# Expert outputs through DRAM by token instead of TensorE spreading, paced zero fill, and two panels split ahead of each item

## The chip, the cores and the metric

The kernel runs on one core of a Trainium2 chip. The metric is the device time of one execution in microseconds, in the median of several runs. TensorE (PE) multiplies, VectorE (DVE) and ScalarE (ACT) prepare operands and read results out of PSUM, SyncE (SP) issues most transfers, GpSimd (POOL) issues a few, and 16 DMA engines move the data between HBM and the on-chip memory SBUF.

## The reference

The program is a chain of four layers on 256 tokens of width 1024. The first block has two layers: a hybrid mixer (RWKV-7 scan, two convolutions, gated and summed) with a layer norm, then in layer 0 a dense SwiGLU of inner width 2816 and in layer 1 a mixture of eight experts, each with a layer norm behind it. The second block has two attention layers, each with a squared-ReLU MLP. All of it is float32. The part that the change touches is the mixture of experts:

```python
def _moe_swiglu(x, w_router, w_gate, w_up, w_down):
    logits = (xf @ w_router).astype(jnp.float32)
    top_logit, top_idx = lax.top_k(logits, TOP_K)          # TOP_K = 2
    top_w = jax.nn.softmax(top_logit, axis=-1)
...
    def expert_block(args):
        xs, e = args
        return (jax.nn.silu(xs @ w_gate[e]) * (xs @ w_up[e])) @ w_down[e]

    yb = lax.map(expert_block, (xb, block_expert))
    y_rows = yb.reshape(n_rows, d) * row_weight[:, None].astype(x.dtype)
    out = jnp.zeros_like(xf).at[row_token].add(y_rows)
```

Each token's output is thus the sum of two expert rows, each times its softmax weight. It is added to ALPHA times the token and goes into a layer norm.

## The kernel before

**Precision.** A float32 product is made of three matmuls in a faster format: each operand is written as a high part and a low part, and hi·hi, lo·hi and hi·lo are added in PSUM (`mm3`, lines 1205 to 1211; its first product goes through `mm`, line 364). ACT makes the high part of a weight panel with a copy ("widens" it, line 2005), DVE subtracts it for the low part ("splits" it, line 2850), and PE may use the panel then.

**Panels.** All weights lie in DRAM as 460 panels of 128 x 2048 numbers, 1 MiB each. SP loads them in order of use. In the experts' part there are seven places for raw panels (three in `ring`, three in `ring_more`, one in `xT`) and four for high parts (three in `ring_hi`, one in `xT_hi`). A place is free for the next panel when the counter `panel_used` has passed the panel that was in it; PE raises the counter with the first matmul of the panel that follows.

**Dense feed-forward of layer 0** (about 300 to 472 us). It uses a ring of three places only: a panel is loaded, cast and split by DVE (lines 2951 and 2953) and used. One chunk is three panels: gate, up and down. At its start POOL writes zeros into the DRAM buffer `routed_x` (line 3399), in one DMA of 6 MiB.

**Experts of layer 1** (about 802 to 1590 us). The tokens of an expert are handled in items of up to 128 rows; the number of items is found on the chip, and this input has 8. One item takes 33 panels: for each of 11 chunks two gate-up panels of 12 matmuls each (`wide`), and one down panel of 12 matmuls (`last`). The order is 0,0,1,1,2,2,down 0,3,3,down 1 and so on. Between the two gate-up panels of chunk s PE turns the hidden tile of chunk s-1 (`turn`). Near the end of an item, in chunk 10, PE also turns the 128 token rows of the next item (`turn_next`), which SP has fetched from `routed_x`, and the next item's `in_slot` one-hot tile, which says what token belongs in which row. ACT and DVE then make `xe_hi` and `xe_lo` of them.

**Outputs of an item before the change.** The down products end in banks 2 and 3. ACT copies them to `y_hi` (line 2024, two halves), DVE makes `y_lo` (line 2871), and PE multiplies them with the one-hot tile `spread` (`scatter`, lines 1331 and 1332): four matmuls of 512 columns for the first half after the first chunk of the next item, four for the second half in chunk 3. That puts the rows of the item at their tokens. DVE adds each result times the token's weight to `acc` (line 2877, four operations of 512 columns an item). The last item's are spread after the loop.

**What each engine does at an item's beginning.** The item body of PE, ACT and DVE is a hardware loop over the first 7 items, followed by a copy of the body for the last one. ACT's body starts with widening gate-up panel 1 (the second of chunk 0), then the first half of the outputs, panel 2, a one-element Silu that brings in the table set, the second half of the outputs, panel 3, and the `silu` of chunk 0. DVE's splits follow the same order. The instruction stream has an ACT_TABLE_LOAD at two places of the loop's body: ahead of its first copy, and ahead of the one-element Silu.

**The start of the experts' part.** DVE computes the routing, loads two numbers into registers, and makes `one_hot`. PE gathers item 0's tokens with it (`gather`, line 1308). DVE then computes the rows in `routed_x` to which each token goes (`route_rows`), sets `acc` to ALPHA times the tokens, and splits panel 0. POOL scatters the tokens into `routed_x` with four indirect DMAs. ACT widens panel 0 beside the gather, panel 1 only as the first thing of the item loop.

## Time and profile before

| | us |
|---|---|
| median of 3 runs | 2289.98 |
| lowest, highest | 2286.58, 2302.31 |
| profiled execution, its own time | 2287.82 |
| span of its profile | 2285.8 |
| PE busy (share of the span) | 2234.8 (98%) |
| DVE busy | 1811.1 (79%) |
| ACT busy | 1058.9 (46%) |
| POOL busy | 13.7 (1%) |
| TensorE clock granted, mean | 0.992 |

The span runs from the first to the last instruction in the profile. The engines wait for each other by semaphores; an idle time is put down to what released it. Matmuls overlap: a matmul of 512 columns is shown as 0.39 us long, while the next one starts about 0.23 us after it. So the distance between two starts is the cost, and a busy share of 98% does not mean that PE has no time to lose.

### The profile page before, as it was taken

What the parts mean: (1) busy time and instruction counts of PE and PEld (TensorE: products, weight loads), DVE (VectorE), ACT (ScalarE), POOL (GpSimd) and SP (SyncE); (2) the same over time, 40 slices, a digit from 0 to 9 for tenths busy, and PEclk for the clock granted to TensorE, in tenths of its full rate; (3) what the DMA queues carried; (4) which work ended last, traced back from release to release, by engine and by line L of the source; (5) the groups of instructions that cost most, each with busy time, mean ns of one, the idle gap of its engine ahead of it and who ended that gap; (6) DMA issues with size and microseconds to landing.
All of it is one profiled execution on the core that took longest, in us unless ns stands there. A gap on an engine that the chain in (4) does not pass through costs nothing.

```text
span 2285.8 us, 39519 instructions
## 1 busy us (share of the span) xinstructions
PE 2234.8 (98%) x15724; PEld 1937.8 (85%) x15724; DVE 1811.1 (79%) x1989; ACT 1058.9 (46%) x1257; POOL 13.7 (1%) x20
## 2 busy tenths in 40 slices
PE   9999999999999999999999999999999999999999
PEld 8999889989899878878788787877888999888998
DVE  4885777778866698988989889897878877578776
ACT  5435410034445377776877768775464100243000
POOL 0000000000000000000000000000000000000000
PEclk9999999999999999999999999999999999999999
DMA  5333465533334499999999999996512555322554
GB/s 209 122 113 115 162 255 206 185 145 130 113 112 148 194 372 347 357 362 359 362 344 380 343 361 354 355 374 239 204 72 75 185 186 189 140 93 94 192 191 149
DMA packets 71903, 507.80 MB, mean 222 GB/s; under 512 B 7808, under 2 KB 7936, under 8 KB 12400
## 3 DMA queue, kind: packets, MB, share of 16 engines
q1 hardware_dynamic: 68240, 489.77, 57.7%
q0 software_dynamic: 3552, 16.44, 1.9%
q8 instruction: 84, 1.38, 0.2%
q14 instruction: 27, 0.22, 0.0%
HBM read 496.74 MB, written 9.44 MB: 221 GB/s over the span
## 4 chain that ended last, share of the span: by engine, by line
PE 80%; DVE 9%; ACT 5%; DMA 3%; issue 2%; DVEq 0%; SPq 0%; ACTq 0%
PE wide L364 27%; PE wide L1210 22%; PE wide L1211 22%; DMA ring<-in_weights 2%; DVE ring_lo L2342 2%; ACT mix_hi L1736 1%; PE wide L1547 1%; DVE ring_lo L2953 1%; PE wide L1291 1%; ACT ring_hi L2005 1%; PE wide L1031 1%; PE wide L1533 1%; DVE ring_hi L2951 0%; ACT xe_hi L2019 0%; PE wide L1023 0%
## 5 line engine op out<-in xcount | busy, mean ns | idle before, releaser
L364 PE MATMUL wide<-ring_hi,hT_hi 128*128 128x512 f32 x664 | 263.6, 397 | 7.4 <-DVE ring_lo L2953 4.2
L1211 PE MATMUL wide<-ring_hi,hT_lo 128*128 128x512 f32 x664 | 261.8, 394 | 0.0
L2850 DVE TENSOR_TENSOR ring_more_lo<-ring_more,ring_hi 128x2048 fp32r<-128x2048 f32 x96 | 219.8, 2290 | 43.6 <-ACT ring_hi L2005 42.0
L364 PE MATMUL wide<-mix_xT_hi,mix_hi 128*128 128x256 f32 x816 | 238.4, 292 | 12.6 <-DVE ring_lo L2342 9.7
L364 PE MATMUL wide<-xT_hi,ring_hi 128*128 128x256 f32 x864 | 243.3, 282 | 3.0 <-DVE xT_lo L2336 1.6
L1961 ACT ACTIVATE gate_s<-wide 128x512 f32<-128x512 f32 x43 | 25.8, 600 | 474.4 <-PE wide L1211 474.4
L1211 PE MATMUL wide<-xT_hi,ring_lo 128*128 128x256 f32 x864 | 242.8, 281 | 0.0
L1210 PE MATMUL wide<-xT_lo,ring_hi 128*128 128x256 f32 x864 | 242.5, 281 | 0.0
L2850 DVE TENSOR_TENSOR ring_lo<-ring,ring_hi 128x2048 fp32r<-128x2048 f32 x96 | 219.7, 2289 | 23.1 <-ACT ring_hi L2005 22.0
L1211 PE MATMUL wide<-mix_xT_hi,ring_lo 128*128 128x256 f32 x832 | 234.4, 282 | 0.0
L1210 PE MATMUL wide<-xT_lo,mix_hi 128*128 128x256 f32 x816 | 230.4, 282 | 0.0
L364 PE MATMUL wide<-ring_hi,xe_hi 128*128 128x512 f32 x544 | 218.8, 402 | 1.4 <-DVE ring_more_lo L2850 1.1
L2953 DVE TENSOR_TENSOR ring_lo<-ring,ring_hi 128x2048 fp32r<-128x2048 f32 x94 | 215.5, 2293 | 3.2
L2342 DVE TENSOR_TENSOR ring_lo<-ring,mix_hi 128x2048 fp32r<-128x2048 f32 x60 | 137.3, 2288 | 101.1 <-ACT mix_hi L1736 100.7
L1211 PE MATMUL wide<-ring_hi,xe_lo 128*128 128x512 f32 x544 | 214.9, 395 | 0.0
L1210 PE MATMUL wide<-ring_lo,hT_hi 128*128 128x512 f32 x536 | 210.3, 392 | 0.0
L2005 ACT ACTIVATE ring_hi<-ring_more 128x2048 fp32r<-128x2048 f32 x96 | 184.3, 1920 | 51.2 <-PE wide L364 50.0
L2005 ACT ACTIVATE ring_hi<-ring 128x2048 fp32r<-128x2048 f32 x96 | 184.1, 1917 | 30.5 <-PE wide L364 30.5
L2951 DVE CAST ring_hi<-ring 128x2048 fp32r<-128x2048 f32 x94 | 115.3, 1227 | 102.9 <-DMA ring<-in_weights 102.9
L364 PEld LDWEIGHTS wide<-mix_xT_hi,mix_hi 128*128 128x128 f32 x816 | 155.1, 190 | 22.4 <-DVE ring_lo L2342 16.0
L364 PEld LDWEIGHTS wide<-xT_hi,ring_hi 128*128 128x128 f32 x864 | 163.2, 189 | 6.5 <-DVE ring_lo L2953 2.7
L1210 PEld LDWEIGHTS wide<-xT_lo,ring_hi 128*128 128x128 f32 x864 | 162.8, 188 | 1.6
(545 smaller groups left out, 4941.5 us busy)
## 6 DMA issues: line engine op xcount, KB each, us to landing
ring<-in_weights SPq DMA_DIRECT2D x316, 1024.0 KB, 4.8
ring_more<-in_weights SPq DMA_DIRECT2D x120, 1024.0 KB, 6.1
xT<-in_weights SPq DMA_DIRECT2D x24, 1024.0 KB, 6.8
routed_x<-xe_tm POOLq DMA_DIRECT2D x1, 6144.0 KB
ln_row<-in_ln_rows POOLq DMA_DIRECT2D x4, 1024.0 KB, 5.3
xe_tm<-routed_x SPq DMA_DIRECT2D x8, 512.0 KB, 7.3
x_tm<-in_x SPq DMA_DIRECT2D x1, 1024.0 KB, 5.4
qkT<-in_mem POOLq DMA_DIRECT2D x1, 1024.0 KB, 5.5
```

Source lines behind the costliest of these rows:

```text
L364: ins = self.pe.matmul(out, lhsT, rhs, start=start, stop=stop)
L1031: straight = pe.matmul(bank[b][hs, h * CHUNK:(h + 1) * CHUNK], lhs[hs, h, :], chunk_ident[hs] if rhs is None else rhs[hs, h, :], start=Tru ...
L1210: pe.matmul(out, lhsT[0], rhs[1], start=False, stop=False)
L1211: return pe.matmul(out, lhsT[1], rhs[0], start=False, stop=stop)
L1291: ins = pe.transpose(bank[6 + s % 2][:, m * CAP:(m + 1) * CAP], h_tm[:, s % 2, m * P:(m + 1) * P], ident)
L1533: ins = pe.transpose(o, p[:, starts[0]:starts[0] + P], ident)
L1961: act.activation(gate_s[:, slot, :, :], b[:].rearrange("p (m t) -> p m t", m=2), func).then_inc(sems["out"], 1)
L2005: act.activation(panel_hi(k), w, ACT.Copy).then_inc(S["panel_wide"], 1)
L2342: tt_(ring_lo[:, g % RING, :], ring[:, g % RING, :], mixer_hi[hi_slot(i)].bitcast(F32), ALU.subtract).then_inc(S["panel_split"], 1)
L2850: tt_(lo, w, panel_hi(k).bitcast(F32), ALU.subtract).then_inc(S["panel_split"], 1)
L2951: copy(ring_hi[:, slot, :], ring[:, slot, :]).then_inc(S["split_hi"], 1)
L2953: tt_(ring_lo[:, slot, :], ring[:, slot, :], ring_hi[:, slot, :].bitcast(F32), ALU.subtract).then_inc(S["split"], 1)
```

## The change

Only the last item is still spread by TensorE. For the others, ACT copies the outputs to the plain tile `y_tm`, SP stores it by rows in `routed_x` (one item further down than the item's tokens' old place; the buffer grows by one item), and in the last item DVE computes the two row numbers and weights of each token (`output_rows`), POOL fetches the rows by token with four indirect DMAs into `y_rows`, and DVE adds them to `acc` in chunks 7 to 10 (`add_rows`). ACT and DVE take panel 1 of the next item ahead of the loop's end, in front of the outputs. Before the first item, ACT widens panels 0 and 1 during the routing, the routing's Exp table set is brought in early, and DVE computes `route_rows` and `acc` only after panel 1. The zero fill is 13 DMAs of 512 KiB, each waiting for two more panels of the dense feed-forward to be used.

```diff
@@ SP, in the loop over items 1 to n_items - 1
                 for k in range(PER_ITEM):
                     place, _, sem, _ = moe_panel(k, item)
+                    if k == OUTPUTS_AT:
+
+                        sp.wait_ge(S["y_sb"], 2 * item + 2)
+                        sp.dma_start(routed_items[bass.ds(item, 1)].rearrange("a p d -> p (a d)"), y_tm[:]).then_inc(S["y_stored"], 16)
                     if k == TOKENS_AT:
 
+                        sp.wait_ge(S["y_stored"], item * 16)
                         sp.wait_ge(S["routed_mm"], item + 1)
-                        sp.dma_start(xe_tm[:], routed_items[bass.ds(item + 1, 1)].rearrange("a p d -> p (a d)")).then_inc(S["xe_in"], 16)
+                        sp.dma_start(xe_tm[:], routed_items[bass.ds(item + 2, 1)].rearrange("a p d -> p (a d)")).then_inc(S["xe_in"], 16)
@@ PE
                     wide(0, 0, item)
                     wide(1, 0, item)
-                    scatter(item, 0)
+                    pe.wait_ge(S["spread"], 1)
...
                         wide(1, s, item)
-                        if s == SECOND_HALF:
-                            scatter(item, 1)
                         if s >= 2:
                             if s == 2:
-                                pe.wait_ge(S["y_lo"], 2 * item + 2)
+                                pe.wait_ge(S["y_sb"], 2 * item + 2)
                             last(s - 2, item)
@@ PE, turn_next: the two transposes of in_slot are gone
-                    for tt in range(TT):
-                        ins = pe.transpose(bank[1][:, tt * P:(tt + 1) * P], in_slot[:, tt, :], ident)
@@ ACT
                 def item_act(item, more):
 
-                    widen(GATE_UP[1], 0, item)
-                    y_out(item, 0)
+                    act.activation(stat[:, 63:64], cst[:, 0:1], ACT.Silu)
...
                     tokens_hi(item + 1)
-                    act.activation(spread[:], bank[1][:, 0:T].rearrange("p (t k) -> p t k", t=TT), ACT.Copy).then_inc(S["spread"], 1)
                     widen("down", FF_CHUNKS - 1, item)
                     hidden_hi(FF_CHUNKS - 1, item)
                     if more:
-                        widen(GATE_UP[0], 0, item + 1)
...
+                        for half in range(2):
+                            widen(GATE_UP[half], 0, item + 1)
+                        for h in range(2):
+                            y_out(item, h)
@@ DVE, item body
+                        if not more:
+                            if s == 0:
+                                output_rows()
+                            elif s == STORED_AT:
+                                outputs_stored(item)
+                            elif s >= FF_CHUNKS - TOP_K * TT:
+                                add_rows(*divmod(s - (FF_CHUNKS - TOP_K * TT), TT))
@@ DVE, new: one of the functions; output_rows is 12 operations of at most 16 columns, in 5 steps that wait for one another
+            def add_rows(k, tt):
+                dve.wait_ge(S["y_back"], 16 * TOP_K * TT)
+                stt(acc[:, tt, :], y_rows[:, k, tt, :], route_w[:, k, tt:tt + 1], acc[:, tt, :], ALU.mult, ALU.add).then_inc(S["dve_step"], 1)
@@ POOL
-                    pool.dma_start(routed_x.rearrange("(i p) d -> p i d", p=CAP), xe_tm[:].unsqueeze(1).to_broadcast([P, ITEMS + 1, D])).then_inc(S["x_routed"], 16)
+                    for i in range(ITEMS + 2):
+                        pool.wait_ge(S["panel_used"], BEFORE_FFN + 2 * i + 2)
+                        pool.dma_start(routed_items[i], xe_tm[:]).then_inc(S["x_routed"], 16)
```

The first place at which the order of instructions changes is ACT's, where one item goes over into the next. In the kernel before, the body of ACT's loop begins so (`ring_hi` and `xT_hi` are high parts, `stat` is the one-element Silu, `y_hi` the outputs):

```order
L2005 ACT_TABLE_LOAD
L2005 ACTIVATE ring_hi<-ring_more 128x2048 [waits panel_used]
L2023 REGISTER_ALU
L2024 ACTIVATE y_hi<-wide 128x512 [waits y_half]
L2004 REGISTER_ALU [waits panel_landed_more_2]
L2005 ACTIVATE ring_hi<-ring_more 128x2048 [waits panel_used]
L2036 ACT_TABLE_LOAD
L2036 ACTIVATE stat<-cst 128x1
L2024 ACTIVATE y_hi<-wide 128x512 [waits y_whole]
L2003 ISA
L2005 ACTIVATE xT_hi<-ring 128x2048 [waits panel_used,panel_landed0]
```

In the changed kernel the same body ends with these rows (panels 0 and 1 of the next item, then its predecessor's outputs):

```order
L1998 ACTIVATE ring_hi<-ring_more 128x2048 [waits panel_used]
L1997 REGISTER_ALU [waits panel_landed_more_1]
L1998 ACTIVATE ring_hi<-ring_more 128x2048 [waits panel_used]
L2024 ACTIVATE y_tm<-wide 128x512 [waits y_half]
L2024 ACTIVATE y_tm<-wide 128x512 [waits y_whole]
L2058 REGISTER_ALU
L2058 COMPARE_AND_BRANCH
```

and its body begins with these, to which the branch goes back:

```order
L2032 ACT_TABLE_LOAD
L2032 ACTIVATE stat<-cst 128x1
L1996 ISA
L1997 ISA [waits panel_landed_more_2]
L1998 ACTIVATE ring_hi<-ring_more 128x2048 [waits panel_used]
L1996 ISA
L1998 ACTIVATE xT_hi<-ring 128x2048 [waits panel_used,panel_landed0]
```

One of the two table loads of the body is gone, and the other one stands ahead of panel 2 now instead of behind it. The body's copy for the last item has no table load in either kernel.

The second place is DVE's, before the first item. Before the change, from the register loads to the loop (`ring_more_lo` is the split of panel 0, `xe_lo` the tokens of item 0):

```order
L2843 TENSOR_LOAD table_i
L2843 ISA x2
L2881 MEMSET item_by 128x2
L2883 TENSOR_SCALAR one_hot<-cst,item_pos 128x128 x2
L2825 SCALAR_TENSOR_TENSOR route_row<-tiles,moe_pos 128x16
...
L2886 TENSOR_SCALAR acc<-x_tm 128x2048 [waits routes]
L2850 TENSOR_TENSOR ring_more_lo<-ring_more,ring_hi 128x2048 [waits panel_wide,acc_read]
L2864 TENSOR_TENSOR xe_lo<-wide,xe_hi 128x512 [waits xe_hi]
L2864 TENSOR_TENSOR xe_lo<-wide,xe_hi 128x512
```

In the changed kernel, from the tokens of item 0 to the first split of the loop, which is that of panel 2:

```order
L2892 TENSOR_TENSOR xe_lo<-wide,xe_hi 128x512
L2878 TENSOR_TENSOR ring_more_lo<-ring_more,ring_hi 128x2048 [waits panel_wide]
L2956 TENSOR_LOAD table_i
L2956 ISA x2
L2958 TENSOR_TENSOR col<-col 128x8 x2
L2829 SCALAR_TENSOR_TENSOR route_row<-tiles,moe_pos 128x16
...
L2960 TENSOR_SCALAR acc<-x_tm 128x2048 [waits routes]
L2961 UNCONDITIONAL_BRANCH
L2961 ISA
L2878 TENSOR_TENSOR ring_more_lo<-ring_more,ring_hi 128x2048 [waits panel_wide]
```

The routing rows, `acc` and one register load have moved from ahead of PE's first panel to between the splits of panels 1 and 2.

## Rows read from the trace of the kernel before

**Rows 1.** Windows: us, busy of PE, PEld, DVE, ACT, POOL, clock, DMA share, GB/s.
```profile
320.00:340.00 20.00, 18.02 (x124) 16.32 (x123) 12.80 (x10) 0.60 (x1) 1.14 (x2) 1.00 1.02 409
...
806.00:820.00 14.00, 13.78 (x61) 11.05 (x62) 12.73 (x11) 12.12 (x13) 0.00 (x0) 1.00 1.00 385
904.00:1002.00 98.00, 97.60 (x438) 78.67 (x437) 87.32 (x67) 73.97 (x65) 0.00 (x0) 1.00 0.94 359
```

**Rows 2.** Timeline of PE from item 0 into item 1: start us, us, instruction.
```profile
889.43 0.38 PE L1319 MATMUL wide<-cst,in_slot 128*128 128x128 f32 x2
889.57 0.48 PE L364 MATMUL wide<-ring_hi,xe_hi 128*128 128x512 f32 x1
...
898.78 0.50 PE L364 MATMUL wide<-ring_hi,hT_hi 128*128 128x512 f32 x1 [0.40 <-DVE hT_lo L2858]
...
901.67 0.39 PE L364 MATMUL wide<-ring_hi,xe_hi 128*128 128x512 f32 x1
...
907.24 0.39 PE L1331 MATMUL wide<-y_hi,spread 128*128 128x512 f32 x1
...
908.17 0.39 PE L364 MATMUL wide<-ring_hi,xe_hi 128*128 128x512 f32 x1
```

**Rows 3.** Timeline of PE and ACT at the end of the last item.
```profile
1584.45 0.50 PE L364 MATMUL wide<-ring_hi,hT_hi 128*128 128x512 f32 x1 [0.40 <-DVE hT_lo L2858]
...
1587.54 0.60 ACT L2024 ACTIVATE y_hi<-wide 128x512 fp32r<-128x512 f32 x1 [0.79 <-PE wide L1211]
```

**Rows 4.** Timeline of ACT and DVE ahead of the last down panel of item 0.
```profile
893.87 0.40 ACT L2048 ACTIVATE spread<-wide 128x256 fp32r<-128x256 f32 x1
...
896.10 2.29 DVE L2850 TENSOR_TENSOR ring_lo<-ring,ring_hi 128x2048 fp32r<-128x2048 f32 x1 [0.24 <-ACT ring_hi L2005]
```

**Rows 5.** Timeline of ACT and DVE at the beginning of item 1.
```profile
899.46 1.92 ACT L2005 ACTIVATE ring_hi<-ring_more 128x2048 fp32r<-128x2048 f32 x1
...
902.10 1.92 ACT L2005 ACTIVATE ring_hi<-ring_more 128x2048 fp32r<-128x2048 f32 x1 [0.23 <-PE wide L364]
904.03 1.28 ACT L2036 ACT_TABLE_LOAD   x1
905.33 0.20 ACT L2036 ACTIVATE stat<-cst 128x1 f32<-128x1 f32 x1
...
904.22 2.28 DVE L2850 TENSOR_TENSOR ring_more_lo<-ring_more,ring_hi 128x2048 fp32r<-128x2048 f32 x1
```

**Rows 6.** Timeline of ACT, DVE, PE and POOL at the start of the experts' part.
```profile
791.81 0.60 ACT L2105 ACTIVATE mem_kv<-wide 128x512 f32<-128x512 f32 x1 [6.37 <-PE wide L364]
...
793.48 0.06 DVE L2881 MEMSET item_by<- 128x2 f32 x1 [1.73 <-issue]
...
796.24 2.29 DVE L2850 TENSOR_TENSOR ring_more_lo<-ring_more,ring_hi 128x2048 fp32r<-128x2048 f32 x1
...
794.02 5.47 PE L1308 MATMUL wide<-one_hot,x_tm 128*128 128x128 f32 x32 [2.31 <-DVE one_hot L2883]
...
802.07 0.49 PE L364 MATMUL wide<-ring_hi,xe_hi 128*128 128x512 f32 x1 [0.32 <-issue]
...
806.22 0.51 PE L364 MATMUL wide<-ring_hi,xe_hi 128*128 128x512 f32 x1 [1.12 <-DVE ring_more_lo L2850]
...
795.81 1.28 POOL L3412 DMA_INDIRECT routed_x<-x_tm,route_i  x1 [14.75 <-DVE route_i L2834]
```

**Rows 7.** Waits of SP's queue between 806 and 1590 us: total us, times, longest.
```profile
SPq L790 <- PE wide L364: 540.7, 224, 5.0
```

**Rows 8.** Timeline of ACT in the dense feed-forward: the end of chunks 2 to 4.
```profile
333.00 0.60 ACT L1961 ACTIVATE gate_s<-wide 128x512 f32<-128x512 f32 x1 [16.58 <-PE wide L1211]
353.88 0.60 ACT L1961 ACTIVATE gate_s<-wide 128x512 f32<-128x512 f32 x1 [20.29 <-PE wide L1211]
370.77 0.60 ACT L1961 ACTIVATE gate_s<-wide 128x512 f32<-128x512 f32 x1 [16.29 <-PE wide L1211]
```

**Rows 9.** Timeline of DVE at the mixer's end: two multiply-adds of 512 columns.
```profile
765.29 1.28 DVE L2659 SCALAR_TENSOR_TENSOR x_tm<-x_tm,wide 128x512 f32<-128x512 f32 x2 [3.79 <-PE wide L1211]
```

More of the change, by code:

```diff
@@ L1340, in moe_pe @@
                 gather().then_inc(S["routed_mm"], 1)
-                pe.wait_ge(S["spread"], 1)
-                nothing = spread[:].rearrange("p t k -> p (t k)")
-                for b, sem in ((2, "y_half"), (3, "y_whole")):
-                    for h in range(2):
-                        ins = pe.matmul(bank[b][:, h * T:(h + 1) * T], spread[:, 0, :], nothing, start=True, stop=True)
-                    ins.then_inc(S[sem], 1)
+                pe.wait_ge(S["one_hot"], 2)
+                for tt in range(TT):
+                    ins = pe.transpose(bank[1][:, tt * P:(tt + 1) * P], in_slot[:, tt, :], ident)
+                ins.then_inc(S["slot_turned"], 1)
                 keep_busy(bank[0][:, 0:P], 8)
@@ L1991, in memory_tokens, with widen_expert @@
                     ins.then_inc(S["mem_xT"], 1)
+            def widen_expert(part, s, item):
+                k = moe_order(part, s)
+                w, _, sem, n = moe_panel(k, item)
+                act.wait_ge(sem, n * 16)
+                act.wait_ge(S["panel_used"], item * PER_ITEM + (BEFORE_MOE + k - HI.back(k) + 1))
+                act.activation(panel_hi(k), w, ACT.Copy).then_inc(S["panel_wide"], 1)
             def moe_act():
+                widen = widen_expert
                 act.wait_ge(S["items_ready"], 1)
@@ L2923, in item_dve @@
                     if more:
-                        split_panel(GATE_UP[0], 0, item + 1)
+                        for half in range(2):
+                            split_panel(GATE_UP[half], 0, item + 1)
                 split_panel(GATE_UP[0], 0, 0)
+                last_item = dve.value_load(table_i[0:1, ITEMS + 2:ITEMS + 3], min_val=N_EXPERTS - 1, max_val=ITEMS - 1)
+                for tt in range(TT):
+                    ins = ts_(in_slot[:, tt, :], count, item_pos[:, tt, bass.ds(last_item, 1)], None, ALU.is_equal)
+                ins.then_inc(S["one_hot"], 1)
                 tokens_lo(0)
+                split_panel(GATE_UP[1], 0, 0)
+                n_items = dve.value_load(table_i[0:1, 0:1], min_val=N_EXPERTS, max_val=ITEMS)
+                for f in ("g", "b"):
+                    tt_(col[:, COLS[f"both_{f}"]], col[:, COLS[f"ln2_{f}1"]], col[:, COLS["attn_norm0"]], ALU.mult)
+                route_rows()
+                ts_(acc[:], x_tm[:], ALPHA, None, ALU.mult)
                 with dve.Fori(0, last_item) as item:
```

141 lines of the change are left out of this document (74 added, 67 removed).

## Prediction

> **What bounds the kernel now.** I looked at the granted clock and the waits first, then at windows over the experts' part, then at the timeline of PE, ACT and DVE where one item goes over into the next, at the start of the part and at its end. In an item PE is busy for 97.6 of 98 us at full clock, DVE for 87, ACT for 74, and the DMA engines for 0.94 of the time [rows 1]. From the last down panel of item 0 to that of item 7 it is (1584.45 - 898.78) / 7 = 97.95 us an item [rows 2, 3]. So PE sets the pace there, and what PE no longer does is worth its full price, as long as DVE, ACT and the transfers still deliver in time. The dense feed-forward is PE's too, with a chunk of 370.77 - 353.88 = 16.89 us, except for the chunk that ends at 353.88: it took 20.88 us [rows 8], while the DMA engines were full at 409 GB/s [rows 1].
>
> **Zero fill.** The one slow chunk lies where the 6 MiB are written. It costs 20.88 - 16.89 = 3.99 us. In pieces of 512 KiB, one for every two panels (11.3 us), a piece takes 0.52 MB / 385 GB/s = 1.4 us of the engines [rows 1], and two panels need 5.4, so that they stay under two thirds full. The ring of three gives a panel little lead, so a delay of 1.4 us might still show in places. Between -4.3 (all, and a little of the chunk before it) and -2.0 (half of it comes back); I take -4.0.
>
> **An item's relief.** Four spreading matmuls take 908.17 - 907.24 = 0.93 us [rows 2]; eight are 1.86. The two transposes of `in_slot` take 0.14, with the slow matmul behind them (0.48 long) 0.2 [rows 2]. ACT no longer makes `spread`, for which DVE waited 0.24 us ahead of the last down panel's split [rows 4]; PE's 0.40 us wait for `hT_lo` behind it [rows 2] shrinks by that. Together 2.3 us.
>
> **A new wait at an item's head.** The ACT rows decide it. Let t be the start of the last down panel, 898.78 now, 898.54 with the 0.24. PE starts the next item at t + 2.89 and wants its panel 2 two panels later; two panels are 907.24 - 901.67 = 5.57 us, so at t + 8.46 = 907.00 [rows 2]. Up to now ACT widened panel 2 at 902.10, the table load came behind it, and four spreading matmuls lay between [rows 2, 5]. In the changed order ACT does panel 1 (about 899.1 to 901.0, when its place is free), the first half of the outputs, and the second half when the last matmul is through: 1587.54 - 1584.45 = 3.09 after t [rows 3], 901.63, plus 0.58, is 902.21. Then 1.28 of table load, and 0.13 to the next copy [rows 5]: panel 2 is widened from 903.6 to 905.55 and split from 905.6 to 907.9. PE waits 0.9 us and loses 0.1 at restarting: 1.0 us. This happens in items 1 to 6. The last item's body has no table load; there panel 2 is split at about 906.6, in time. What follows (panel 3, the product) is in time after such a wait.
>
> A page speaks against this size. The Trainium skill's "ScalarE: Activation LUTs", section "What ACT_TABLE_LOAD costs", gives 1283 ns for the load plus about 1380 ns of drain for each switch of set. Here the load is 1.28 us and the next instruction starts 0.02 us behind its end (904.03 + 1.28 to 905.33) [rows 5], so no drain shows. By the page the wait would be 2.4 us an item, six times 1.4 more.
>
> **The last item.** DVE has `output_rows` behind panel 3's split: 12 small operations in five steps, 2 us by the steps of routing ahead of `acc` (796.24 - 793.48 = 2.76 with `acc` and one-hots in it) [rows 6]. Without the spreading matmuls PE wants panel 3 about 0.5 us before its split ends (DVE takes it behind the product, at 908.2, and is through at 910.5; PE wants it at 910.05), and panel 4 at 913.35, while DVE ends it at 914.8: 0.5 + 1.5 us. The four `add_rows` are 1024 columns each, 1.28 us by two of 512 [rows 9] (bounds 0.6 and 1.5). Three fall into chunks in which DVE has time (98 - 87.3 us idle in an item, and 5 us of outputs and accumulating gone [rows 1]); the fourth stands right ahead of the last tokens, the last split and `hT_lo`, which PE already waits for, so it costs 1.25. The item: -2.3 + 2.0 + 1.25 = +0.95.
>
> **The start.** PE's gather waited for DVE's `one_hot`, behind 1.73 us for two register loads and a chain that waited for Exp's table load; both go out of its way, and then PE has to wait for the copy that ends at 791.81 + 0.60 = 792.4: about 792.5 for 794.02, -1.5 (at least -0.6, if PE's own register load is late) [rows 6]. The first panel follows at 800.6 for 802.07. Panel 2 doesn't come sooner by more than that: behind the tokens DVE has a split (2.29), a register load (half of 1.73), the routing rows and `acc` (2.76 less 0.4 of one-hots), small things (0.3), and panel 2's split (2.29): 8.1, 8.0 us after PE's start, where PE wants it after 5.57. Before, PE had panel 2 after 4.15 (with the 1.12 wait) + 2.79 + 0.93 = 7.9 [rows 2, 6]. So the wait for panel 1, the spreading and the four matmuls with zeros turn into a wait of 2.4 us, and the start gives -1.5 in all. POOL's scatter of 2.1 MB starts some 11 us later than 795.81 and falls into a stretch in which the DMA engines are full at 385 GB/s anyway [rows 1, 6]. It is 5.4 us of their time; the first panels land about 3.7 us sooner in exchange. I put +0.7 on it (0 to 4). The rest of item 0: -0.93 - 0.2 - 0.24 = -1.4.
>
> **Transfers in the items.** The store adds 0.52 MB. An item moves 98 us x 359 GB/s = 35.2 MB; 35.7 MB at 385 GB/s are 93 us [rows 1], under the new 96.6. SP waits 540.7 of 784 us for PE to give a place back [rows 7], so it is places, not engines, that hold panels back. SP's store stands ahead of panel 8 and waits for ACT's second output half (902.2), which is there long before panel 8's place. I put the store at nothing: its cover is that raw panels wait for ACT, and in the middle of an item split ones for PE. The fetch of 2.1 MB in the last item has the same cover, and may cost up to 3.
>
> **Sum**, against the profiled execution's own 2287.82 us (2.2 under the median): -4.0 (fill) -1.5 (start) -1.4 + 0.7 (item 0) - 6 x (2.3 - 1.0) = -7.8 (items 1 to 6) + 0.95 (item 7) = -13.05, so **2274.8 us**, 0.7% under the median of 2289.98. A difference under 1% of it, 22.9 us, counts as the same here.
>
> **Rivals.**
> - *The relief comes whole.* ACT gets to panel 2 in time (the outputs overlap with the load, or the load is short when its set is already in), and DVE keeps up in the last item. For it: PE is full and nearly all its waits in the items are 0.4 us. Against it: the table load is 1.28 us in every item though nothing new is loaded, and DVE's work is in order. 2274.8 - 6.0 - 2.0 = 2266.8.
> - *The table load costs more*, or something else at the item's head comes late, such as panel 3: a wait of 2.4 us instead of 1.0 takes all relief of items 1 to 6. 2274.8 + 6 x 1.4 = 2283.2. The page above says so; the rows don't.
> - *Transfers become the bound (the slower side).* If the cover is used up, each store delays PE by its 1.4 us and the 0.93 us that PE now wants panels sooner in chunk 3 aren't won: +2.3 in 7 items, and 5.4 each for the late scatter and the fetch. 2274.8 + 16.1 + 5.4 + 4.7 = 2301.0. It decides when a panel's landing plus copy plus split is later than PE by more than the lead that DVE has in mid-item. For it: 0.94 busy, and 1.00 in the first item. Against it: the average still fits, and SP waits for PE.
> - *The fill still hurts* in pieces: +2, within the range.
>
> **Chances.** Forecast 0.50; whole relief 0.20; table load or another late panel (2281 to 2288) 0.22; transfers 0.08. The range takes the whole relief's 2267 with some room below, and on the other side most of the third case: 2263 to 2284. Faster by over 1% means under 2267.1, about half of the second case's spread and a little of the first: 0.18. Slower by over 1% would need over 2312.9: 0.02. The same: 0.80.
>
> **What would show it.** The chunk that ends near 354 at 16.9 us. Distances of 96.6 us between the items' last down panels in the loop. On PE, at each item head, a wait of about 0.9 us for the split of panel 2, behind an ACT_TABLE_LOAD that ends at t + 5. At the start, a gather at 792.5 and 2.4 us of waiting for panel 2. In the last item, waits for panels 3 and 4 and one of over 1 us for `hT_lo`. I am wrong if ACT or DVE wait for landings in mid-item and PE behind them, or if the item heads show no wait.

## The result, and the profile of the changed kernel

The changed kernel takes 2271.95 us in the median of 8 runs (2269.08 to 2281.59), the kernel before 2287.90 beside it (8 runs, 2284.80 to 2302.31): a ratio of 0.9929, with an interval of 0.9911 to 0.9946. That is 16 us less, or 0.7%. The profiled execution spans 2269.8 us where that of before spanned 2285.8, at the same mean granted clock of 0.992. The forecast was 2274.8, "the same" by the bound of 1%, so the kernel came out 2.9 us faster than forecast.

From the page of the changed kernel, its head and the traffic:

```profile
span 2269.8 us, 39254 instructions
...
PE 2220.1 (98%) x15642; PEld 1925.0 (85%) x15642; DVE 1784.5 (79%) x1935; ACT 1046.5 (46%) x1242; POOL 33.2 (1%) x36
...
HBM read 498.84 MB, written 13.63 MB: 226 GB/s over the span
```

PE is still busy for 98% of a shorter span, so it remains the bound. What the change traded is in the last line: 13.63 MB are written in place of 9.44, by seven stores of 0.52 MB and one more block of zeros.

**The zero fill.** ACT's timeline at the ends of the feed-forward's chunks, which answers to [rows 8]:

```profile
332.74 0.60 ACT L1960 ACTIVATE gate_s<-wide 128x512 f32<-128x512 f32 x1 [16.54 <-PE wide L1221]
349.89 0.60 ACT L1960 ACTIVATE gate_s<-wide 128x512 f32<-128x512 f32 x1 [16.55 <-PE wide L1221]
366.73 0.60 ACT L1960 ACTIVATE gate_s<-wide 128x512 f32<-128x512 f32 x1 [16.24 <-PE wide L1221]
```

The two chunks take 17.15 and 16.84 us where they took 20.88 and 16.89. From 333.00 and 370.77 of before to 332.74 and 366.73 here, (370.77 - 333.00) - (366.73 - 332.74) = 3.78 us are gained in two chunks.

**Windows**, with the columns of [rows 1], over a stretch of the fill and over an item in the loop:

```profile
320.00:334.00 14.00, 13.99 (x108) 13.18 (x107) 10.13 (x9) 0.60 (x1) 1.59 (x3) 1.00 0.92 336
...
885.00:982.00 97.00, 96.10 (x429) 77.14 (x428) 83.61 (x59) 72.54 (x62) 0.00 (x0) 1.00 0.96 368
```

While the zeros are written PE is busy all the time, and the DMA engines are at 0.92, where they were at 1.02 with PE busy for 18.02 of 20 us. In the loop PE stands idle for 0.9 us of each 97, and the DMA engines are busy 0.96 at 368 GB/s (0.94 at 359 before).

**The start of the experts' part**, answering to [rows 6]: PE's gather, its first panel and its panel 2, and between them DVE's work.

```profile
788.33 3.81 PE L1318 MATMUL wide<-one_hot,x_tm 128*128 128x128 f32 x32 [0.84 <-ACT mem_kv L2106]
794.71 0.49 PE L365 MATMUL wide<-ring_hi,xe_hi 128*128 128x512 f32 x1 [0.57 <-DVE xe_lo L2892]
801.42 0.50 PE L365 MATMUL wide<-ring_hi,xe_hi 128*128 128x512 f32 x1 [0.86 <-DVE ring_more_lo L2878]
...
794.50 2.28 DVE L2878 TENSOR_TENSOR ring_more_lo<-ring_more,ring_hi 128x2048 fp32r<-128x2048 f32 x1
796.70 0.23 DVE L2958 TENSOR_TENSOR col<-col 128x8 f32<-128x8 f32 x2
...
799.08 2.29 DVE L2878 TENSOR_TENSOR ring_more_lo<-ring_more,ring_hi 128x2048 fp32r<-128x2048 f32 x1
```

The gather's wait fell from 2.31 to 0.84 us. The wait of 1.12 us for panel 1 is gone. PE now waits 0.86 us for panel 2; the prediction had put 2.4 there.

**One item into the next**, answering to [rows 2, 5]: PE's last down panel of item 0, panel 2 of item 1, and the last down panel six items on; then ACT and DVE at the head of item 1.

```profile
888.62 0.50 PE L365 MATMUL wide<-ring_hi,hT_hi 128*128 128x512 f32 x1
898.01 0.50 PE L365 MATMUL wide<-ring_hi,xe_hi 128*128 128x512 f32 x1 [0.77 <-DVE ring_more_lo L2878]
...
1468.72 0.50 PE L365 MATMUL wide<-ring_hi,hT_hi 128*128 128x512 f32 x1
...
890.98 0.58 ACT L2024 ACTIVATE y_tm<-wide 128x512 f32<-128x512 f32 x1
891.71 0.60 ACT L2024 ACTIVATE y_tm<-wide 128x512 f32<-128x512 f32 x1 [0.15 <-PE wide L1221]
892.33 1.28 ACT L2032 ACT_TABLE_LOAD   x1
893.62 0.20 ACT L2032 ACTIVATE stat<-cst 128x1 f32<-128x1 f32 x1
893.73 1.90 ACT L1998 ACTIVATE ring_hi<-ring_more 128x2048 fp32r<-128x2048 f32 x1
...
895.66 2.29 DVE L2878 TENSOR_TENSOR ring_more_lo<-ring_more,ring_hi 128x2048 fp32r<-128x2048 f32 x1 [2.27 <-ACT ring_hi L1998]
```

An item takes (1468.72 - 888.62) / 6 = 96.68 us, where it took 97.95. The new wait is there at each head: DVE stands 2.27 us for ACT's copy of panel 2, which came behind two output halves and the table load, and PE stands 0.77 us for DVE. The six waits of PE sum to 4.6 us.

**The last item**: PE's panel 4 and its last down panel, and DVE's last two additions.

```profile
1484.17 0.50 PE L365 MATMUL wide<-ring_hi,xe_hi 128*128 128x512 f32 x1 [0.60 <-DVE ring_lo L2878]
1567.48 0.50 PE L365 MATMUL wide<-ring_hi,hT_hi 128*128 128x512 f32 x1 [2.05 <-DVE hT_lo L2886]
...
1561.81 1.28 DVE L2911 SCALAR_TENSOR_TENSOR acc<-y_rows,route_w,acc 128x1024 f32<-128x1024 f32 x1
1563.60 1.29 DVE L2892 TENSOR_TENSOR xe_lo<-wide,xe_hi 128x512 fp32r<-128x512 f32 x2 [0.52 <-DVE acc L2911]
```

It takes 1567.48 - 1468.72 = 98.76 us, 2.1 more than an item of the loop, although it has no wait of 0.77 us at its head. The waits shown are the 2.05 us for `hT_lo` and the 0.60 for panel 4. ACT, which waited for no landing of a weight panel in the items of the loop, waits 6.0 us for landings here, behind the fetch of the rows.

The account of the 16.0 us between the two profiled executions: fill with what lies around it -3.9, mixer of layer 1 -3.2, start -1.5, item 0 -1.5, items 1 to 6 -7.6, last item +0.8, the rest +1.0. The mixer and the rest weren't touched: there TensorE's granted clock differs between the two executions. Rows of windows of before, and then one of the changed kernel, show it (the whole stretch of the changed kernel is 6.8 us long, against 10.2 and 3.4 before):

```profile
507.90:518.00 10.10, 10.10 (x25) 6.79 (x24) 0.10 (x1) 3.76 (x9) 0.00 (x0) 0.50 0.01 2
736.60:739.80 3.20, 3.19 (x15) 3.19 (x16) 3.17 (x6) 1.28 (x2) 0.00 (x0) 0.50 0.48 105
```

```profile
506.00:512.00 6.00, 6.00 (x16) 4.35 (x16) 0.00 (x0) 1.75 (x6) 0.00 (x0) 0.50 0.01 3
```

PE is busy all through such a stretch, at 1.2 GHz in place of 2.4, and its work takes longer: matmuls of 512 columns that follow one another start 0.43 us apart in one (1565.12 to 1565.55 in a0_changed_again) and 0.23 us apart outside (1568.28 to 1568.51 in the changed kernel). Such stretches differ from execution to execution of one kernel. f1_changed_beside, the changed kernel again, has a mean of 0.57 from 506 to 518 us where before had 0.58, so the 3.2 us of the mixer don't belong to the change. This became the chief difficulty of the experiments.

### The profile page after: what moved, and what is told of

The parts are those of the page before. It is cut to its first block, busy times and chain, and to the rows that moved or that the text cites. A ratio compares the mean times of both kernels' runs of the same rounds, so it can differ in the third digit from the quotient of the medians.

```text
span 2269.8 us, 39254 instructions
## 1 busy us (share of the span) xinstructions
PE 2220.1 (98%) x15642; PEld 1925.0 (85%) x15642; DVE 1784.5 (79%) x1935; ACT 1046.5 (46%) x1242; POOL 33.2 (1%) x36
## 3 DMA queue, kind: packets, MB, share of 16 engines
HBM read 498.84 MB, written 13.63 MB: 226 GB/s over the span
## 4 chain that ended last, share of the span: by engine, by line
PE 80%; DVE 10%; ACT 5%; issue 3%; DMA 2%; DVEq 0%; ACTq 0%; SPq 0%
PE wide L365 27%; PE wide L1220 21%; PE wide L1221 21%; DVE ring_lo L2346 2%; DMA ring<-in_weights 1%; ACT mix_hi L1735 1%; ACT ring_hi L1998 1%; DVE ring_more_lo L2878 1%; PE wide L1546 1%; PE wide L1301 1%; PE wide L1041 1%; DVE ring_lo L2878 1%; PE wide L1532 1%; DVE ring_lo L2986 1%; DVE xe_lo L2892 0%
```

## The experiments

**Two measures beside the median.** The first is the distance between the items' last down panels on PE: 96.68 or 96.69 us in the mean of every profiled execution of the changed kernel. The second is the span times the mean granted clock, which takes off about what the half clock added (not exactly, since a slow stretch costs nothing where PE waits anyway). For example 2269.8 x 0.992 = 2251.7. Over all runs of a kernel its median is called "at full clock" below. The kernel before had 2265.7, 2267.1, 2266.8 and 2267.2 at full clock in four groups of 27, 13, 12 and 9 runs, and medians of 2287.65, 2286.36, 2287.21 and 2286.22. The last two columns of the table come from one profiled execution of each kernel.

| kernel | runs | median | at full clock | item of the loop | last item |
|---|---|---|---|---|---|
| changed | 8 | 2271.95 | 2251.6 | 96.68 | 98.76 |
| a0_changed_again | 10 | 2282.08 | 2252.0 | 96.69 | 99.42 |
| f1_changed_beside | 5 | 2274.71 | 2253.9 | 96.69 | 99.07 |
| e1_fill_at_once | 10 | 2277.81 | 2256.9 | 96.69 | 98.76 |
| e2_head | 10 | 2271.03 | 2247.2 | 96.02 | 98.93 |
| e3_last_item | 6 | 2273.07 | 2253.6 | 96.69 | 100.45 |
| e4_start | 4 | 2271.18 | 2252.3 | 96.68 | 98.84 |
| e5_all_three | 4 | 2270.33 | 2247.0 | 96.06 | 100.35 |
| e6_matmuls_back | 10 | 2283.12 | 2260.0 | 97.62 | 99.73 |
| e7_store_twice | 4 | 2273.13 | 2252.2 | 96.69 | 98.77 |
| e8_store_four | 1 | 2278.86 | 2261.1 | 97.57 | 100.75 |
| e9_all_corrected | 7 | 2272.36 | 2244.1 | 96.06 | 96.23 |
| f2_all_corrected | 4 | 2266.31 | 2246.0 | 96.06 | 97.89 |

**a0_changed_again** is the changed kernel, for the scale of the others.

> The changed kernel once more, as the measure for the other runs on this chip. My sum gave 13.05 us less than before; the first profile shows 16.0 less in the span. Of these, 3.2 lie in the mixer of layer 1, which the change does not touch, where TensorE's granted clock was at half for 6.83 us instead of 10.24 + 3.41. Theory A (the clock's half stretches fall differently in each execution and are no part of the change): this profile has them at other places or of other lengths, and the distances that the change sets are the same: 16.9 us for the chunk of the zero fill, 96.68 us an item, 98.76 for the last. Theory B (the change itself moves the clock): the mixer is again about 3 us shorter than before.

Its median came out 10 us above the first one (ratio to the kernel before 0.9974, interval 0.9948 to 1.0000), with single runs from 2269.17 at a clock of 0.994 to 2295.91 at 0.978. At full clock it is 2252.0 against 2251.6. The distances in the loop are the same, but the last item took 99.42 us where 98.76 was expected: 0.6 us build up in delays of about 0.1 us each between 1531 and 1554, and the wait for `hT_lo` is 2.12. ACT waited 7.0 us for landings in it, against 6.0; that this is the cause isn't shown. f1_changed_beside has 99.07. So the length of the last item is known to some 0.7 us only. And since medians of this kernel move by 10 us with the clock alone, differences under that are read from the two other measures.

**e1_fill_at_once** puts the fill back in one piece.

```diff
-                    for i in range(ITEMS + 2):
-                        pool.wait_ge(S["panel_used"], BEFORE_FFN + 2 * i + 2)
-                        pool.dma_start(routed_items[i], xe_tm[:]).then_inc(S["x_routed"], 16)
+                    pool.dma_start(routed_x.rearrange("(i p) d -> p i d", p=CAP), xe_tm[:].unsqueeze(1).to_broadcast([P, ITEMS + 2, D])).then_inc(S["x_routed"], 16 * (ITEMS + 2))
```

> The changed kernel with the zero fill as one DMA of 6.5 MiB at the old place. Theory: the pacing is worth what the one slow chunk cost, 3.7 to 4.3 us, so this is 3.7 to 4.3 us over the changed kernel and the chunk that now ends at 349.9 ends about 4 us later. Rival (pieces cost something too, or the gain comes from elsewhere): under 2 us.

The first of four waits on PE that this brings back, in its timeline:

```profile
334.82 0.50 PE L365 MATMUL wide<-ring_hi,hT_hi 128*128 128x512 f32 x1 [1.72 <-DVE ring_lo L2986]
```

With 0.58 at 341.22, 0.50 at 347.63 and 0.69 at 354.24 they sum to 3.49 us. The chunk that ends at 353.67 took 20.53 us, and the chunk ends at 472.64 where the changed kernel's ends at 468.03, 4.6 us later. At full clock it is 4.9 to 5.3 slower than the first two groups of the changed kernel and 3.0 slower than f1_changed_beside. The fill is worth what the slow chunk of [rows 8] said, and perhaps a little more than the 3.7 to 4.3 expected.

**e6_matmuls_back** has eight matmuls in each item again, of the size of the spreading ones, into banks that are free and read by nobody: four behind panel 1's products, where they stood, and four in chunk 3. They compute nothing that is used.

```diff
+                def as_before():
+                    for i in range(4):
+                        pe.matmul(bank[4 + i // 2][:], spread[:, i // 2, :], xe_hi[:, 0:4, :].rearrange("p k c -> p (k c)"), start=True, stop=True)
...
+                    as_before()
...
+                        if s == 3:
+                            as_before()
```

> The changed kernel with eight matmuls of 512 columns in each item at the two places where the spreading stood (their result is used by nobody). Theory: the first four fall into PE's wait of 0.77 + 0.1 us at the item's head and cost 0 to 0.2, the second four cost 0.93: 7 x 0.95 plus 0.9 to 1.9 in item 0 and the last, 8 to 9 us in all, about half of 64 x 0.2325 = 14.9. Rival (PE's work is worth its full price, and the wait at the head comes on top): +14.9.

The last down panels of items 0 and 1 on PE:

```profile
885.44 0.50 PE L365 MATMUL wide<-ring_hi,hT_hi 128*128 128x512 f32 x1
983.05 0.50 PE L365 MATMUL wide<-ring_hi,hT_hi 128*128 128x512 f32 x1
```

The item takes 97.61 us, 0.93 more than in the changed kernel, and no wait is left at its head. PE's busy time in it is 97.48 against 95.79: the eight matmuls are 1.69 us, and 0.77 of that went into time in which PE stood waiting before. At full clock the kernel is 8.4 slower than the first group of the changed one, within the 8 to 9 expected. So nearly half of what TensorE is relieved of in an item was not gained by the change. The ratio of medians, 0.9987 (0.9960 to 1.0013), says less, since the clocks of the ten runs lie between 0.981 and 0.993. The profiled run, at 0.982, had PE at half clock for 44 us in a row in a stage behind the experts:

```profile
2042.30:2086.50 44.20, 43.42 (x150) 35.01 (x149) 22.33 (x61) 14.87 (x33) 0.00 (x0) 0.50 0.00 1
```

**e2_head** takes ACT's two output halves from ahead of the table load to behind panel 2's copy, so that panel 2 comes 1.2 us sooner. (The two bank semaphores get a first increment of their own for this, by transposes that the kernel did anyway to keep PE busy.)

```diff
                     for s in range(FF_CHUNKS):
                         if s + 1 < FF_CHUNKS:
                             widen(GATE_UP[0], s + 1, item)
+                        if s == 0:
+                            for h in range(2):
+                                y_out(item, h)
...
-                        for h in range(2):
-                            y_out(item, h)
```

> The changed kernel with ACT's two output copies behind panel 2 instead of ahead of the loop's branch; the table load stays the first thing in the body. So that the first item has outputs to copy, PE writes banks 2 and 3 with transposes in place of eight idle ones. Theory (the wait of 0.77 us at each item head comes from ACT's chain outputs, table load, panel 2): panel 2 is widened about 1.3 us sooner, the wait of items 1 to 6 goes or shrinks to 0.1 to 0.3 at panel 3, and the time falls by 3 to 5 us. Rival (it is the DVE's order or the transfers that make PE wait there): the wait stays, same time within 1 us.

ACT at the head of item 1:

```profile
893.89 1.28 ACT L2035 ACT_TABLE_LOAD   x1
...
895.30 1.90 ACT L2001 ACTIVATE ring_hi<-ring_more 128x2048 fp32r<-128x2048 f32 x1
897.10 1.06 ACT L2027 ACTIVATE y_tm<-wide 128x512 f32<-128x512 f32 x2
```

The last down panel before it starts at 891.42, so panel 2's copy comes 3.88 us behind it, where it came 893.73 - 888.62 = 5.11 behind. The 0.77 us at the heads are gone, and 0.13 of idle time remains ahead of panel 3. The item takes 96.02 us, 0.66 less, and the kernel at full clock 4.4 to 4.8 less than the first two groups of the changed one: six items by 0.66 is 4.0. The queue ahead of panel 2 was the cause, and the table load itself can stay. The median, 2271.03, shows nothing of this beside the 2271.95 of the first group, and 11 us beside the 2282.08 of its own.

**e4_start** has the tokens and panel 1's split of item 0 behind the register load, the routing rows and `acc` again.

```diff
-                tokens_lo(0)
-                split_panel(GATE_UP[1], 0, 0)
                 n_items = dve.value_load(table_i[0:1, 0:1], min_val=N_EXPERTS, max_val=ITEMS)
...
+                tokens_lo(0)
+                split_panel(GATE_UP[1], 0, 0)
```

> The changed kernel with the routing rows, acc and the register load ahead of the tokens of item 0, where DVE idles for 4 us, instead of behind panel 1's split. Theory: PE's wait for panel 2 in item 0 (0.86 us) goes and the routed rows are scattered some 7 us sooner, so 0.9 to 1.2 us less. Rival (the gather or the tokens then come later by it): no gain, 0 to +1.

The wait for panel 2 is gone. From the first panel to the last down panel of item 0 it is 889.00 - 795.72 = 93.28 us, against 93.91: 0.63 less, and not the 0.9 to 1.2 expected. DVE has time ahead of the tokens, since there the changed kernel has it wait 4.0 us for ACT's `xe_hi`; the routing rows fit into that. At full clock (2252.3) 0.6 us can't be seen.

**e3_last_item** moves `output_rows` from chunk 0 to chunk 3, and the four additions from chunks 7 to 10 to chunks 6 to 9.

```diff
-                            if s == 0:
+                            if s == 3:
...
-                            elif s >= FF_CHUNKS - TOP_K * TT:
-                                add_rows(*divmod(s - (FF_CHUNKS - TOP_K * TT), TT))
+                            elif FF_CHUNKS - 1 - TOP_K * TT <= s < FF_CHUNKS - 1:
+                                add_rows(*divmod(s - (FF_CHUNKS - 1 - TOP_K * TT), TT))
```

> The changed kernel with the row numbers and weights computed in chunk 3 instead of 0, and the four additions in chunks 6 to 9 instead of 7 to 10. Theory (in the last item only DVE's order costs): PE's wait of 2.05 us ahead of the last down panel goes down to 0.13 and the 0.60 at panel 4 goes, so 2.5 to 2.7 us less than the changed kernel; the last item takes 96.1 us instead of 98.76. Rival (the fetch of 2.1 MB makes panels late in the last item): the distance stays above 97.5, and PE or ACT wait for landings.

That missed. The last item grew to 100.45 us. The rows of POOL, DVE and PE say why:

```profile
1510.45 3.00 POOL L3453 DMA_INDIRECT y_rows<-routed_x,route_i  x1 [704.87 <-DVE route_i L2866]
...
1532.45 1.28 DVE L2911 SCALAR_TENSOR_TENSOR acc<-y_rows,route_w,acc 128x1024 f32<-128x1024 f32 x1 [4.62 <-DMA y_rows<-routed_x,route_i]
...
1536.20 0.56 PE L365 MATMUL wide<-ring_hi,xe_hi 128*128 128x512 f32 x1 [2.47 <-DVE ring_more_lo L2878]
1567.85 0.50 PE L365 MATMUL wide<-ring_hi,hT_hi 128*128 128x512 f32 x1 [0.23 <-DVE hT_lo L2886]
```

The wait for `hT_lo` fell from 2.05 to 0.23 as expected, but in chunk 6 the fetched rows hadn't landed. The last of four fetches leaves POOL at 1519.54 + 2.41 = 1521.95, and DVE's wait for the rows ends 10.5 us later, at 1532.45. DVE stood 4.62 us in order behind them, and PE 2.47. In the changed kernel the last fetch leaves POOL at 1521.34 and the first addition is at 1540.03, 18.7 us behind it, and doesn't wait. **e5_all_three**, e2, e3 and e4 together, went with it: 96.06 us an item, and 100.35 for the last, with a wait of 2.34 us at 1529.96. The gains of the three did not add up to the 7 to 9 us expected.

> The three reorderings together: outputs behind panel 2, the last item's additions a chunk sooner, routing rows ahead of the tokens. Theory: the gains add up, 7 to 9 us less than the changed kernel, items at about 95.8 us, 2263 to 2265 us in all. Rival (with PE's waits gone, the transfers become the bound): items stay above 96.3 and ACT waits for landings; 2267 or more.

**e9_all_corrected** puts this right: `output_rows` in chunk 2, and the conversion of the indices, which releases the fetches, a chunk sooner.

```diff
-STORED_AT = 4
+STORED_AT = 3
...
-                            if s == 3:
+                            if s == 2:
```

> The head of the items and the start reordered as in e2_head and e4_start, and the last item once more: output_rows in chunk 2, the conversion of the indices (and so the fetch's release) in chunk 3 rather than 4, add_rows in chunks 6 to 9. In e3_last_item VectorE waited 4.62 us at 1532.45 for the fetched rows, which landed 22 us after the first of the four fetches was issued (1510.45), and TensorE then lost 2.47 us to the panel behind it. Theory A (the additions stood ahead of the landing, nothing else): the fetches go out near 1498 to 1503 on the scale of e3, land by 1523, before chunk 6's addition near 1530; no wait for ring_more_lo in chunk 6, at most 0.3 us for hT_lo at the end; the last item 96.1 to 96.5 us where the changed kernel has 98.76; items 1 to 6 96.0 each; the profiled span, at a clock like that of the changed kernel's profile (0.992), 2262 to 2264; median 2263 to 2268. Rival B (the earlier fetch meets VectorE with no time left, or the fetched rows displace panels, as the queue is at its fullest in chunks 3 to 5): a wait for a panel of 1 us or more in chunks 3 to 6, and the last item 98 or longer. Rival C (the clock of TensorE gives back what the waits lost): distances as in A, and a median not below 2269.

The first fetch, the first addition, and the last down panels of items 6 and 7:

```profile
1500.29 3.00 POOL L3456 DMA_INDIRECT y_rows<-routed_x,route_i  x1 [702.49 <-DVE route_i L2869]
...
1526.61 1.28 DVE L2914 SCALAR_TENSOR_TENSOR acc<-y_rows,route_w,acc 128x1024 f32<-128x1024 f32 x1
...
1464.56 0.50 PE L365 MATMUL wide<-ring_hi,hT_hi 128*128 128x512 f32 x1
1560.79 0.50 PE L365 MATMUL wide<-ring_hi,hT_hi 128*128 128x512 f32 x1 [0.33 <-DVE hT_lo L2889]
```

The last item takes 96.23 us, the expected 96.1 to 96.5, and the profiled span is 2262.2 at 0.992. At full clock the kernel is 7.5 to 7.9 under the first two groups of the changed one. The distances give 6 x 0.62 = 3.7 in the loop, 0.6 at the start as in e4, and 2.5 in the last item, 6.8 in all. But the median, 2272.36, with clocks from 0.985 to 0.992, was above the 2263 to 2268 expected and no better than the changed kernel's first 2271.95. So both kernels were run once more in the same rounds:

> The changed kernel, a third time, in the same rounds as f2_all_corrected, since e9_all_corrected's distances were as theory A said (items 96.06, the last 96.23 us) and its median was not (2272.36 with granted clocks of 0.985 to 0.992, its profiled execution 2264.02 at 0.992). Theory A (TensorE's clock varies from execution to execution whatever the schedule): clocks of both kernels spread alike; this one's span times its clock 2251 to 2253 as before (2251.6 and 2252.0), its median anywhere in 2270 to 2283.

> The corrected version beside the changed kernel. Theory A: span times clock 2244 to 2246, 7 to 8 us under f1_changed_beside, clocks spread like those of f1, and a median 5 to 9 us under it. Rival C (the fuller TensorE loses the gain to its clock): its clocks lie 0.002 to 0.003 under those of f1, and the two medians are within 3 us.

There it is 2266.31 against 2274.71, 8.4 us apart, 0.9909 (0.9894 to 0.9924) and 0.9942 (0.9929 to 0.9956) of the kernel before, and 7.9 apart at full clock. The clocks were 0.991 to 0.993 and 0.988 to 0.993: the fuller TensorE did not run at a lower clock in these rounds. Its last item was 97.89 here, 1.66 more than in e9. Most of that comes in chunk 6, and it starts ahead of the first addition at 1526.18: a panel lands late, ACT waits for it, DVE for ACT, and PE for DVE.

```profile
1519.07 1.92 ACT L2001 ACTIVATE ring_hi<-xT 128x2048 fp32r<-128x2048 f32 x1 [3.97 <-DMA xT<-in_weights]
...
1521.02 2.29 DVE L2881 TENSOR_TENSOR xT_lo<-xT,ring_hi 128x2048 fp32r<-128x2048 f32 x1 [3.69 <-ACT ring_hi L2001]
...
1523.69 0.44 PE L1301 MATMUL wide<-cst,gate_s 128*128 128x128 f32 x2 [0.68 <-DVE gate_s L2885]
```

In e9 ACT waited 2.83 us at this place, and PE not at all. At 1529.93, behind the addition, PE waits another 0.21 us. So in the last item, where the rows are fetched beside the panels, the landings are close to costing time, and in this execution they did. Why they differ between the two isn't shown.

**e7_store_twice** and **e8_store_four** store each item's outputs once and three times more, to a place that nobody reads.

```diff
+                        for i in range(1):
+                            sp.dma_start(beside[i], y_tm[:]).then_inc(S["y_stored"], 16)
...
-                        sp.wait_ge(S["y_stored"], item * 16)
+                        sp.wait_ge(S["y_stored"], item * 32)
```

> The changed kernel with the outputs of an item stored twice, once more into a buffer that nobody reads: 0.52 MB more for each of 7 items. Theory (the transfers are covered: raw panels lie some time before ACT takes them, and split ones before PE does): 0 to +0.5 us, items at 96.7. Rival (the DMA engines are the bound in the items): 1.4 us for each of 7 items, +9.5 us.

> The changed kernel with three further copies of each item's outputs stored to a place that nobody reads (y_tm is stored four times: 2 MB an item in place of 0.5 MB). One copy more (e7_store_twice) left the items at 96.7 us. An item moves about 35.5 MB of reads at 369 GB/s in 96.7 us, with the engines of the transfers busy 96% in the stretch shown. Theory A (the transfers have room only because the window includes waiting and a share of headroom near 4%): 1.57 MB more is 4.4% more bytes, 4.3 us at 369 GB/s, about what 4% of 96.7 us gives; the items grow by 0 to 2 us. Rival B (writes go beside reads and cost them nothing): items stay at 96.7. Rival C (transfers are the bound already and e7 was within the rings' slack): items grow by 3.5 us or more, to over 100.

The items' windows, first of e7, then of e8:

```profile
885.00:982.00 97.00, 96.11 (x429) 77.20 (x428) 83.78 (x59) 72.72 (x62) 0.00 (x0) 1.00 0.96 375
```

```profile
887.00:984.00 97.00, 94.81 (x423) 76.16 (x422) 82.12 (x58) 71.56 (x61) 0.00 (x0) 1.00 0.96 381
...
915.60 0.44 PE L1304 MATMUL wide<-cst,gate_s 128*128 128x128 f32 x2 [1.30 <-DVE gate_s L2885]
```

One store more leaves the items' length as it was (96.69), though ACT, which waited for no landing of a panel in items 1 to 6 of the changed kernel, now waits 10.3 us for landings in these six. With three more it waits 38.2 us. Three more make the items 97.04 to 98.19 long, 97.57 in the mean, and a wait shows in the middle of an item, at 915.60: PE waits for DVE, and DVE has waited 2.96 us for ACT, which waited 3.79 us for a panel to land. In the window shown, PE is busy 94.81 us in place of 96.10. This rests on one run of e8, read by its trace. The transfers have cover for 0.5 MB more and not for 1.6; a copy costs (97.57 - 96.68) / 3 = 0.3 us on the average of the three, well under the 1.4 us that 0.5 MB takes of the engines.

## Why the prediction was right, and where its terms were off

**The fill**, -4.0: -3.9 between the profiles, and e1 shows it as the fill's own.

**Relief of an item**, 2.3 us. By windows from last down panel to last down panel PE's busy time fell from 97.54 to 95.79, 1.75 us (e6: the eight matmuls are 1.69 of it, 0.21 each, and not 1.86), and its idle time ahead of the last down panel from 0.40 to 0.13. That is 2.0, so the term was 0.3 too large.

**New wait at the head**, 1.0 us: measured 0.77. The mechanism was as put: ACT's output halves, the table load, panel 2's copy, DVE's split, PE. Panel 2's split starts 7.04 us after the last down panel where the working had 7.06 (905.6 against 898.54). PE wanted it 898.01 - 0.77 - 888.62 = 8.62 us after the last down panel, not 8.46. The errors of this term and the one above cancel: net 1.27 in place of 1.3 us, and 7.6 in place of 7.8 in six items. The distance forecast was 96.6, measured 96.68. e2 shows that this queue alone made the wait. The Trainium skill, "ScalarE: Activation LUTs", section "What ACT_TABLE_LOAD costs", puts a drain of about 1380 ns on top of the load for every switch to a different set. No run here shows such a drain. At the item's head the load ends at 893.61 and the next instruction starts at 893.62; the set that is loaded there may be the one already in. But where a Sqrt follows Exps in the mixer, at 54.00 us of the changed kernel's profile, the load takes 1.28 us too and the Sqrt starts at 55.29.

**The start**, -1.5: measured -1.5, but the agreement is an accident of the clock. The router's first matmul on PE and panel 2 of item 0 before, then the router's in the changed kernel:

```profile
775.95 3.71 PE L1667 MATMUL wide<-mid,xT 128*128 128x8 f32 x32 [0.32 <-ACT xT L1703]
...
810.05 0.39 PE L364 MATMUL wide<-ring_hi,xe_hi 128*128 128x512 f32 x1
```

```profile
768.86 4.50 PE L1666 MATMUL wide<-mid,xT 128*128 128x8 f32 x32 [0.32 <-ACT xT L1702]
```

Between the two places it was 810.05 - 775.95 = 34.10 us before and 801.42 - 768.86 = 32.56 after. Before, the gather ran at half clock and took 5.47 us in place of 3.81; after, the router did (771.6 to 778.4), which put 19.47 us between its first matmul and the gather. In a0 neither did, and there its rows on PE are:

```profile
767.52 3.71 PE L1666 MATMUL wide<-mid,xT 128*128 128x8 f32 x32 [0.32 <-ACT xT L1702]
...
784.12 3.81 PE L1318 MATMUL wide<-one_hot,x_tm 128*128 128x128 f32 x32 [0.84 <-ACT mem_kv L2106]
790.50 0.50 PE L365 MATMUL wide<-ring_hi,xe_hi 128*128 128x512 f32 x1 [0.57 <-DVE xe_lo L2892]
797.21 0.50 PE L365 MATMUL wide<-ring_hi,xe_hi 128*128 128x512 f32 x1 [0.86 <-DVE ring_more_lo L2878]
```

The gather comes 784.12 - 767.52 = 16.60 us after the router's first matmul, where it was 18.07: -1.47, as put. From the first panel to panel 2 it is 6.71 us where it was 7.98: -1.27, where the sum had +0.1 and so kept the start at -1.5. So the start is worth 2.7 us. What the prediction had wrong is DVE's work between the two splits: from panel 1's split to the end of panel 2's it took 801.37 - 794.50 = 6.9 us, not 8.1, mainly since the register load doesn't show at all (the split ends at 796.78, the next row starts at 796.70), where I had put 0.9 for it. e4 puts another 0.63 us on DVE's order there. The -1.47 of the gather is read from the traces alone; no run took that part of the change back.

**Item 0 behind it**, -0.7 with 0.7 for scatters that come late: -1.5, so the scatters cost nothing that can be seen. ACT waited up to 1.8 us for landings in item 0, and PE not at all.

**The last item**, +0.95: measured +0.8, and +1.5 and +1.1 in a0 and f1. The term for `hT_lo` was 1.25 and came out at 1.9 (2.05 less the 0.13 that is left in the loop): 1.28 for the addition, and 0.52 in which DVE's next instruction waits for its end. The waits for panels 3 and 4 were put at 2.0 and were 0.13 + 0.60. Two errors of opposite sign hide each other here too. e3 and e9 show that both can be had back, if the fetches go out a chunk sooner.

**Transfers**, at nothing: for the stores e7 confirms it, and e8 shows how near the edge was. For the fetch in the last item the cover is thinner: ACT waits 6.0 to 8.4 us for landings there in the changed kernel and in f2, none before the change, and in f2 PE lost time behind it. The rival of 2301 had 2.3 us an item on one store; with four an item pays 0.9.

**The profile's baseline.** The sum, -13.05, was made between profiles. At full clock the difference is 2251.6 against 2265.7 to 2267.2, 14 to 16 us, and for f1, within its own rounds, 2253.9 against 2267.2, 13.3. Between the profiles it is 16.0. Without the mixer's -3.2 and the +1.0 behind the experts, where nothing was changed, it is 13.8, and with the start at full clock (-2.7) 15.0. So these profiles put the change at 15 us, two more than the sum, nearly all of it at the start (-1.2) and in item 0 (-0.8); with the longer last items of a0 and f1 it is 14.3 to 14.7. The range's low side had been meant for the relief coming whole; that did not happen in the changed kernel, and happened in f2.

What stays open: why TensorE's clock falls where it does, and so why a0 had ten runs with a median of 2282; and why the landings in the last item differ between executions of one kernel.

## To carry to other kernels

When the engine that sets the pace is relieved, look at the next thing that the other engines owe it, and in which order they do it: here nearly half of the relief went into one queue on ACT, and moving two copies behind one panel gave most of it back. A result that comes by DMA and is consumed on an engine that works in order must be consumed behind its landing; moving the consumer sooner without the producer costs more than it brings (e3). And a gain below the spread of the clock is read from distances in the trace, or from spans times clock, or in the same rounds, and not from medians of separate rounds.

## What the runs showed of the hardware

One kernel's medians in three groups of rounds were 2271.95, 2282.08 and 2274.71 us, while spans times clock were 2251.6, 2252.0 and 2253.9. The stretches at 0.50 came in part at the same places in all executions (near 30, 505 and 2055 us), in part in some only. They don't follow from the wait ahead of them alone: nine profiled executions have the last item's wait of 2.04 to 2.13 us for `hT_lo`, and behind it four show about 3.4 us at 0.50 and five none. The windows behind that wait, of a0_changed_again and of the changed kernel:

```profile
1564.60:1567.90 3.30, 3.30 (x9) 2.52 (x8) 0.63 (x1) 0.60 (x1) 0.00 (x0) 0.50 0.63 216
```

```profile
1567.60:1571.00 3.40, 3.29 (x14) 2.40 (x15) 0.69 (x1) 1.03 (x2) 0.00 (x0) 1.00 0.50 198
```

Two register loads on DVE left 1.73 us of idle time where they stood alone [rows 6]; one that was queued behind a split of 2.28 us left none. And in e3 the fetched rows were there 10.5 us after the last of four indirect fetches was through at POOL. Each fetch held POOL for 2.4 to 3.0 us there, 1.9 to 3.0 in e9 and 1.0 to 2.7 in the changed kernel.
